# Scaling the attention probabilities on GpSimd ahead of their transposes, in place of scaling the attention output by a transposed inverse

## What is computed

```python
s_own = jnp.where(k_pos[None, None, :] <= q_pos[None, :, None], s_own, NEG_INF)
probs = jax.nn.softmax(jnp.concatenate([s_sel, s_own], axis=-1), axis=-1).astype(v.dtype)
...
return (jnp.einsum('hqnl,hqnld->hqd', p_sel, v_sel)
        + jnp.einsum('hql,hld->hqd', p_own, v_own))
...
mixed = jnp.concatenate([rms_norm(attn_out, attn_out_g[i]),
                         rms_norm(gmlp_out, gmlp_out_g[i])], axis=-1)
h = h + rms_norm(jnp.einsum('bse,ed->bsd', mixed, w_o[i]), mix_post_g[i])
```

## Time and profile before

| | |
|---|---|
| median of 3 runs | 578.59 us (578.13 to 578.95) |
| profiled execution, its own time | 578.39 us |
| its span | 576.7 us |
| TensorE busy | 568.4 us (99%) |
| VectorE busy | 500.4 us (87%) |
| ScalarE busy | 374.9 us (65%) |
| GpSimd busy | 99.3 us (17%) |
| granted TensorE clock | 0.996 of full speed |
| part of the program with the attention | about 102 us to 188 us |

### The profile page before, as it was taken

The page is one execution under the profiler, slowest core; times in us unless marked ns, Lnnn a source line. Parts: engine busy times, 40 slices in busy tenths (PEclk is TensorE's granted clock), DMA queues, the critical chain, the costliest instruction groups (busy, mean ns, idle before and its releaser), DMA issues.

```text
span 576.7 us, 8934 instructions
## 1 busy us (share of the span) xinstructions
PE 568.4 (99%) x3364; PEld 496.2 (86%) x3364; DVE 500.4 (87%) x645; ACT 374.9 (65%) x595; POOL 99.3 (17%) x159
## 2 busy tenths in 40 slices
PE   9999999999999999999999999999999999999995
PEld 8888888888888888999999989999998999988884
DVE  5799986688765988999999989999999899798898
ACT  6886774876555746667565565765666656686784
POOL 0332447000102501001010010011010100015122
PEclk9999999999999999999999999999999999999998
DMA  8982008223103597378476394593774753898833
GB/s 271 350 323 83 0 2 315 88 73 110 39 1 110 157 346 226 74 202 202 71 255 148 73 274 91 148 254 43 240 169 82 257 126 79 323 241 173 220 115 148
DMA packets 28603, 93.73 MB, mean 163 GB/s; under 512 B 3216, under 2 KB 4624, under 8 KB 28304
## 3 DMA queue, kind: packets, MB, share of 16 engines
q1 hardware_dynamic: 20736, 67.64, 33.2%
q0 software_dynamic: 5328, 19.14, 19.2%
q10 hardware_dynamic: 2496, 6.37, 2.9%
HBM read 86.85 MB, written 6.29 MB: 162 GB/s over the span
## 4 chain that ended last, share of the span: by engine, by line
PE 87%; DVE 5%; DMA 3%; ACT 2%; issue 2%; POOL 1%; DVEq 0%; ACTq 0%; POOLq 0%
PE psum L2703 27%; PE psum L2707 26%; PE psum L2708 26%; DMA raw_second<-weights_dram 2%; PE psum L2941 2%; PE psum L2758 2%; PE psum L2921 2%; DVE w_lo L1376 1%; DMA raw<-weights_dram 1%; PE psum L2812 1%; DVE h L1486 1%; PE psum L2772 1%; ACT w_hi L2146 1%; DVE psum L1463 1%; DVE psum L1474 0%
## 5 line engine op out<-in xcount | busy, mean ns | idle before, releaser
L2703 PE MATMUL psum<-t_hi,a_hi 128*128 128x512 f32 x216 | 84.7, 392 | 0.0
L2707 PE MATMUL psum<-t_lo,a_hi 128*128 128x512 f32 x216 | 84.6, 392 | 0.0
L2708 PE MATMUL psum<-t_hi,a_lo 128*128 128x512 f32 x216 | 84.0, 389 | 0.0
L2703 PE MATMUL psum<-w_hi,actT_hi 128*128 128x512 f32 (+1 forms) x178 | 69.7, 391 | 0.0
L2708 PE MATMUL psum<-w_hi,actT_lo 128*128 128x512 f32 (+1 forms) x178 | 68.5, 385 | 0.0
L2707 PE MATMUL psum<-w_lo,actT_hi 128*128 128x512 f32 (+1 forms) x178 | 68.4, 385 | 0.0
L2708 PE MATMUL psum<-sum_hi,up_lo 128*128 128x256 f32 x224 | 63.4, 283 | 0.0
L2707 PE MATMUL psum<-sum_lo,up_hi 128*128 128x256 f32 x224 | 63.4, 283 | 0.0
L2703 PE MATMUL psum<-sum_hi,up_hi 128*128 128x256 f32 x224 | 63.2, 282 | 0.0
L2708 PE MATMUL psum<-actT_hi,up_lo 128*128 128x256 f32 (+1 forms) x200 | 60.0, 300 | 0.0
L2707 PE MATMUL psum<-actT_lo,up_hi 128*128 128x256 f32 (+1 forms) x200 | 60.0, 300 | 0.0
(11 more groups left out here) (290 smaller groups left out, 1465.7 us busy)
## 6 DMA issues: line engine op xcount, KB each, us to landing
raw<-weights_dram SPq DMA_DIRECT2D x40, 512.0 KB, 4.9
raw_o<-weights_dram SPq DMA_DIRECT2D x23, 512.0 KB, 4.4
raw_x<-weights_dram POOLq DMA_DIRECT2D x21, 512.0 KB, 5.5
raw_second<-weights_dram SPq DMA_DIRECT2D x16, 512.0 KB, 4.0
raw_x<-weights_dram SPq DMA_DIRECT2D x9, 512.0 KB, 6.2
qk_raw<-weights_dram SPq DMA_DIRECT2D x8, 512.0 KB, 6.9
raw_o<-weights_dram POOLq DMA_DIRECT2D x7, 512.0 KB, 7.0
raw_second<-weights_dram POOLq DMA_DIRECT2D x6, 512.0 KB, 6.9
```

Source lines behind the costliest of these rows:

```text
L2703: begin = nc.tensor.matmul(out, a_hi, b_hi, start=first, stop=False, skip_group_check=read_between)
L2707: nc.tensor.matmul(out, a_hi, b_lo, start=False, stop=False, skip_group_check=read_between)
L2708: return nc.tensor.matmul(out, a_lo, b_hi, start=False, stop=last, skip_group_check=read_between)
```

## The change

The row sums are inverted unit by unit (`invert`) and not tile by tile. The probabilities are multiplied in place by the inverse of their row's sum before TensorE transposes them: for unit 0 VectorE does it with 8 operations of 128 columns (`scale_first_probs`), for the other ten units GpSimd does it (`scale_probs`), with one operation per head: 4 of 256 columns for each of units 1 and 2, 2 of 384 columns for units 3 to 6, 2 of 512 columns for units 7 to 10. `turn_probs` waits for the scaled probabilities. The repeated inverse, its four transposes per tile, its copy by ScalarE and the multiplication by VectorE are gone. The output of `attend` is now copied from PSUM by ScalarE (`drain_attn`). Several calls change place: on VectorE pairs of `splits` and `attn_lo`, on ScalarE the squares and splits of tile 1, on TensorE one product of `proj(18)` is now ahead of the transposes of unit 0 and one more ahead of its `attend`, and `mean_square(2)` is two products later.

```diff
@@ -995,25 +998,24 @@
                                       psum[:, scores_bank(unit), 0:parts * P].rearrange("p (k q) -> p k q", q=P)
                                       ).then_inc(pt0_drained, 1)
-            def attn_inverse(qt):
-
-                dve.wait_ge(probs_ready, units_until(qt))
-                sums = rowsum[:, PAIRS * qt:PAIRS * (qt + 1), :].rearrange("p a b -> p (a b)")
-                nc.vector.reciprocal(rinv[:], sums).then_inc(inverted, 1)
-                dve.wait_ge(inverted, qt + 1)
-                nc.vector.tensor_copy(inverse.rearrange("p a (b d) -> p a b d", d=DH),
-                                      rinv[:].rearrange("p (a b) -> p a b", b=2)[:, :, :, None]
-                                      .to_broadcast([P, PAIRS, 2, DH])).then_inc(rinv_ready, 1)
-
-            def attn_columns(qt):
-
-                dve.wait_ge(pv_done, units_until(qt))
-                dve.wait_ge(inverse_drained, qt + 1)
-                if qt:
-                    dve.wait_ge(*drained["attn_lo", qt - 1])
-                nc.vector.tensor_tensor(attn[:].rearrange("p (a q) -> p a q", a=PAIRS),
-                                        psum[:, BANK_O, :].rearrange("p (a q) -> p a q", a=PAIRS),
-                                        inverse_turned, ALU.mult).then_inc(attn_ready, 1)
+            def invert(unit):
+
+                qt, pairs = UNITS[unit]
+                dve.wait_ge(probs_ready, unit + 1)
+                first, last = pairs[0], pairs[-1] + 1
+                sums = rowsum[:, PAIRS * qt + first:PAIRS * qt + last, :].rearrange("p a b -> p (a b)")
+                nc.vector.reciprocal(rinv[:, 2 * first:2 * last], sums).then_inc(inverted, 1)
+
+            def scale_first_probs():
+
+                qt, pairs = UNITS[0]
+                n, g = (qt + 1) * P, place_in_group(0)
+                dve.wait_ge(inverted, 1)
+                for s, pair, j in units_heads(0):
+                    part = probs[:, g, s, j * n:(j + 1) * n]
+                    last = nc.vector.tensor_scalar(part, part, rinv[:, 2 * pair + s:2 * pair + s + 1], None,
+                                                   ALU.mult)
+                last.then_inc(first_scaled, 1)
             def attn_sum(qt):
...
@@ -1092,53 +1094,57 @@
             row_maxima(0)
             splits(G_O0 * KD + 2)
+            invert(0)
+            scale_first_probs()
             qkT_lo(6)
             qkT_lo(7)
-            attn_inverse(0)
             drain_pt0(0)
-            attn_columns(0)
             row_maxima(1)
             attn_sum(0)
             row_maxima(2)
             attn_mean(0)
+            invert(1)
             attn_spread(0)
             splits(G_O0 * KD + 4)
-            splits(G_O0 * KD + 6)
-            attn_inverse(1)
+            invert(2)
             attn_scale(0)
             drain_pt0(1)
             drain_pt0(2)
+            splits(G_O0 * KD + 6)
             attn_lo(0)
-            attn_columns(1)
             row_maxima(3)
             attn_sum(1)
             row_maxima(4)
+            invert(3)
             attn_mean(1)
             splits(G_O1 * KD)
             attn_spread(1)
-            splits(G_O1 * KD + 2)
+            invert(4)
             attn_scale(1)
             drain_pt0(3)
             drain_pt0(4)
+            splits(G_O1 * KD + 2)
+            attn_lo(1)
             splits(G_O1 * KD + 4)
-            attn_lo(1)
-
+
+            row_maxima(5)
             splits(G_O1 * KD + 6)
-            row_maxima(5)
             row_maxima(6)
+            invert(5)
             gain_mixed(0, 0)
-            attn_inverse(2)
+            invert(6)
             gain_mixed(0, 1)
             drain_pt0(5)
             drain_pt0(6)
             add_mixed(0)
-            attn_columns(2)
             row_maxima(7)
+            row_maxima(8)
+            invert(7)
             attn_sum(2)
-            row_maxima(8)
+            invert(8)
             attn_mean(2)
             attn_spread(2)
             attn_scale(2)
...
@@ -1148,14 +1154,14 @@
             row_maxima(9)
             row_maxima(10)
+            invert(9)
             gain_mixed(1, 0)
+            invert(10)
             gain_mixed(1, 1)
-            attn_inverse(3)
             add_mixed(1)
             drain_pt0(9)
             drain_pt0(10)
-            attn_columns(3)
             attn_sum(3)
             hn_raw(0)
             hn_raw(1)
...
@@ -1818,11 +1824,12 @@
                                      psum[:, scores_bank(unit) + 1, 0:parts * P].rearrange("p (k q) -> p k q", q=P),
                                      ACT.Copy).then_inc(pt1_drained, 1)
-            def drain_inverse(qt):
-                act.wait_ge(filled, filled1["attnT", qt])
-                nc.scalar.activation(inverse_turned, psum[:, bank1["attnT", qt], :]
-                                     .rearrange("p (a q) -> p a q", a=PAIRS), ACT.Copy).then_inc(inverse_drained, 1)
-                drained["attnT", qt] = (inverse_drained, qt + 1)
+            def drain_attn(qt):
+
+                act.wait_ge(pv_done, units_until(qt))
+                if qt:
+                    act.wait_ge(*drained["attn_lo", qt - 1])
+                nc.scalar.activation(attn[:], psum[:, BANK_O, :], ACT.Copy).then_inc(attn_ready, 1)
             def square_attn(qt):
                 act.wait_ge(attn_ready, qt + 1)
...
@@ -1897,19 +1904,19 @@
             proj_drain(19)
             drain_pt1(1)
             drain_pt1(2)
-            drain_inverse(1)
             attn_hi(0)
+
+            drain_attn(1)
+            square_attn(1)
             splits(G_O1 * KD)
-
-            square_attn(1)
+            softmax(3)
             splits(G_O1 * KD + 2)
-            softmax(3)
             softmax(4)
             square_out(0, 0)
             drain_pt1(3)
             drain_pt1(4)
+            attn_hi(1)
             splits(G_O1 * KD + 4)
-            attn_hi(1)
             splits(G_O1 * KD + 6)
             softmax(5)
...
@@ -2423,13 +2430,35 @@
                 nc.gpsimd.tensor_tensor(rstd_at[:, qt:qt + 1], mean_at[:, qt:qt + 1], minus_half[:, 0:1], ALU.pow
                                         ).then_inc(at_rstd, 1)
+            def scale_probs(unit):
+
+                qt, pairs = UNITS[unit]
+                n, g = (qt + 1) * P, place_in_group(unit)
+                pool.wait_ge(inverted, unit + 1)
+                for s, pair, j in units_heads(unit):
+                    part = probs[:, g, s, j * n:(j + 1) * n]
+                    last = nc.gpsimd.tensor_scalar(part, part, rinv[:, 2 * pair + s:2 * pair + s + 1], None,
+                                                   ALU.mult)
+                last.then_inc(probs_scaled, 1)
+
             attn_rstd(0)
+            scale_probs(1)
+            scale_probs(2)
+            scale_probs(3)
             attn_rstd(1)
+            scale_probs(4)
+            scale_probs(5)
+            scale_probs(6)
             out_rstd(0)
             hidden_rstd(0)
+            scale_probs(7)
+            scale_probs(8)
             attn_rstd(2)
+            scale_probs(9)
             out_rstd(1)
+            scale_probs(10)
             hidden_rstd(1)
+
             def hn_lo(i):
                 t, j = hn_of(i)
                 pool.wait_ge(hn_hi_done, i + 1)
...
@@ -2786,15 +2815,6 @@
                 pe.wait_ge(hn_ready, t + 1)
                 turn(phase1, bank1, ("hT", i), work[:, j, :])
-            def turn_inverse(qt):
-
-                name = ("attnT", qt)
-                pe.wait_ge(rinv_ready, qt + 1)
-                bank_free(phase1, bank1, name)
-                for a in range(PAIRS):
-                    mm = nc.tensor.transpose(psum[:, bank1[name], a * P:(a + 1) * P], inverse[:, a, :], ident[:])
-                mm.then_inc(filled, 1)
-
             def mean_square(qt):
                 pe.wait_ge(at_summed, qt + 1)
                 nc.tensor.matmul(psum[:, BANK_O, W - P:W - P + 1], at_rows[:], mean_of_w[:],
...
@@ -2915,7 +2935,10 @@
                 qt, pairs = UNITS[unit]
                 bank = scores_bank(unit)
-                pe.wait_ge(probs_ready, unit + 1)
+                if unit == 0:
+                    pe.wait_ge(first_scaled, 1)
+                else:
+                    pe.wait_ge(probs_scaled, scaled_by_pool(unit))
                 for s in range(2):
                     for k in range(len(pairs) * (qt + 1)):
                         mm = nc.tensor.transpose(psum[:, bank + s, k * P:(k + 1) * P],
...
@@ -2949,21 +2972,19 @@
             proj(17)
             turn_qk(6)
             turn_qk(7)
-            proj(18, range(0, 2))
+            proj(18, range(0, 3))
             turn_probs(0)
-            proj(18, range(2, 4))
-            turn_inverse(0)
+            proj(18, range(3, 5))
             attend(0)
             scores(1)
             scores(2)
-            proj(18, range(4, KD))
+            proj(18, range(5, KD))
             mean_square(0)
             proj(19)
             turn_scale(0)
             turn_probs(1)
```

(20 more changed lines are left out.)

9 lines of the change are left out of this document (4 added, 5 removed).

## The result

The changed kernel takes 601.8 us (median of 4 runs, 600.25 to 602.47) where the one before takes 578.36 beside it: 1.040 of the time (95% interval 1.038 to 1.042), 23.4 us more. The profiled execution has a span of 600.7 us and a mean granted clock of 0.982 (0.996 before). The forecast was +0.9 us, and the range ended at 583.0.

What follows compares the result with a forecast made beforehand. TensorE, busy 99% of the span, was taken as the bound. The saving of 1.9 us against waits A to F (0.4, 0.5, 0.7, 0.5, 0.4, 0.3) gave +0.9 us, a median of 579.5 us; whole range 577.4 to 583.0.

Steps and rivals of the forecast that it cites:

- A: Wait of TensorE ahead of unit 0's transposes, for VectorE's eight multiplications at 0.20 us each: 0.4 us.
- B: Wait of TensorE ahead of `mean_square(0)`, with three products ahead of it instead of four: 0.4 us, with the semaphore 0.5.
- W: Not forecast: TensorE's wait after VectorE's low parts of the last group's slabs 2 and 3 moved behind copies; 0.7 us.
- The saving: Sixteen transposes of the repeated inverse gone from TensorE: three tiles give back 0.44 us each, tile 2 0.59.
- C: Wait of TensorE ahead of unit 2's transposes, for GpSimd's scaling of units 1 and 2: 0.7 us.
- dearest rival: GpSimd scales at its two-input rate, 0.7, 1.0 and 1.27 us an operation: +10 us, 588.5 us; chance 0.08.
- D: Wait of TensorE ahead of `turn_scale(1)`, tile 1's power being queued behind unit 3's scaling on GpSimd: 0.5 us.
- E: Wait of TensorE ahead of unit 4's transposes, for GpSimd's scaling: 0.4 us.
- F: Wait of TensorE ahead of unit 6's transposes, for GpSimd's scaling: 0.3 us.
- Units 7 to 10 are not late at this price: No wait of TensorE there: units 7 and 8 scaled by 157.9 and 159.4 us, wanted from 160.86 on.
- The turn-taking: One GpSimd operation gets through per VectorE operation while VectorE makes low parts, each moving VectorE on by about 0.65 us.
- the scaling hides: Rival: GpSimd's scaling causes no waits C to F, only A and B remain: 577.2 to 577.6 us; chance 0.18.

Runs made afterwards that it cites:

- fillers: Changed kernel with 220 unread matmuls of 128 bf16 columns laid ahead of the late transposes and of `turn_scale(1)` and `(2)`: 595.22 us, ratio 1.029.
- e_free: Changed kernel without GpSimd's scaling of units 1 to 10, transposes waiting for the reciprocals instead: 578.26 us beside 578.23 of before, ratio 1.000.
- e_tt: Changed kernel with GpSimd scaling by its two-input form, the inverse repeated with a stride of zero: 584.76 us, ratio 1.011.
- m_price: Separate measuring kernel, GpSimd operations alone and beside VectorE's subtractions: multiplication by a scalar alone takes 922, 1242 and 1562 ns for 256, 384 and 512 columns.

## Why the prediction was wrong

- **What bounds the kernel: right.** Each wait of TensorE came back as time. The sum closes without the fillers: e_free is level with before (the 1.9 us saved less A, B and W), and from there to the changed kernel it is 16.3 us at the waits and 8.1 of work at the lower clock, 24.4 by the profiled executions.
- **The saving, 3 x 0.44 + 0.59 = 1.9 us: right**, as e_free's starts show it (1.8).
- **A, 0.4: right.** Eight operations in 1.66 us, 0.2 each, wait 0.4. The 0.20 was a choice between a quarter and the whole of 0.40, so the hit is partly luck. **B, 0.5: right**, 0.25 idle and 0.4 by the starts.
- **C is the step that failed: "I take the first, being nearer in inputs: 0.41 for 256 columns, 0.52 for 384, 0.64 for 512".** Undisturbed it is 0.92, 1.24 and 1.56. The nearness in inputs was no reason at all: the form with one tile and a scalar is dearer than the form with two tiles (1.56 for 1.26 at 512 columns). It went beyond my dearest rival as well (0.7, 1.0 and 1.27), and the range left even that one out. C is 3.5 us (0.99 and 2.51) where I had 0.7, D 1.6 for 0.5, E 1.7 for 0.4, F 2.7 for 0.3, all in idle time; C and F have a second wait, ahead of units 1 and 5, that I did not have.
- **The sums from the price to the waits** were too high, if anything. e_tt has almost the dearest rival's price (0.73, 0.94 and 1.04), for which I had +10 us, and lost 6.5.
- **"Units 7 to 10 are not late at this price": fell with the price.** The power of tile 2 stands behind four operations of 1.57 us, and TensorE waits 2.95 for it; unit 10 adds 2.80.
- **The turn-taking** was the lesser part and came otherwise than I had it. For unit 1 I added 1.3 us for two low parts; they cost 0.6 (1.00 and 1.46 for 0.92 each). At 140.75 one operation waited out two low parts, 1.1 us longer, and that I had as 1.3. By the Trainium skill (SBUF — State Buffer, Who interferes with whom) the two engines share one pair of ports under an exclusive lock; m_price fits that, with 1.43 us for 0.92 beside VectorE's subtractions. In this kernel it comes to 1.7 us of GpSimd's time.
- **The clock: not in the sum at all.** 8.1 us. All my rows came from stretches in which TensorE never waited, at 1.00, and I priced its work at that clock behind waits of 1 to 3 us too.
- **W: not seen.** I wrote out which operations move on VectorE and did not follow the moved low parts into SyncE's queue. 0.7 us in e_free; in the changed kernel, where TensorE is late anyway, 0.2 of it is left (the wait for `w_lo`).
- **The rival "the scaling hides", 577.2 to 577.6,** did not come even with no scaling at all: e_free gave 578.26, because of W.

## What to carry to other kernels

Price an operation by a row of the same form on the same engine; where the trace has none, the bounds from other forms aren't bounds, and a small kernel that measures it is cheaper than the argument. When the bound engine is TensorE, a long wait can cost its own length and then again in clock (here 8.1 us on top of 16.3), so losses grow faster than the overrun. And if work moves to another engine on the path from softmax to transposes, the saved products must be placed anew on TensorE: the same scaling went from +23.4 to -1.1 us by another engine and another order.

## What was unexpected of the hardware

- GpSimd's multiplication of a tile by a scalar per partition: 2.5 ns a column (1562 ns for 512), with a constant 1487, product of two tiles 1261, copy 613; with one operand at stride zero 1040. Why the form with fewer inputs is the dearest is open.
- GpSimd beside VectorE: when VectorE issues low parts back to back, one operation of GpSimd can wait for both (2.31 us for one that takes 1.24), while VectorE's took 1.40, no longer than alone. Beside 16 subtractions in a row each operation of 256 columns took 1.43 us for 0.92.
- TensorE's granted clock was 0.77 over 13 us in which it was busy throughout, behind waits of 0.99 and 2.51 us, and 1.00 when fillers stood in those waits. The lower level came also behind the waits of 1.09 and 1.57 (units 5 and 6), of 2.95 and of 2.80, but not behind those of 1.62 and 1.67. In e_tt, with waits of at most 1.2 us, it stayed at 0.997 over the span.
